# FFN of a two-layer encoder: the gate and the up product of a row block alternate matmul by matmul

## What is computed

```python
def swiglu(h, w_gate, w_up, w_down):
    return (jax.nn.silu(h @ w_gate) * (h @ w_up)) @ w_down

x = x + swiglu(rms_norm(x, f_norm_g[layer]), f_w_gate[layer], f_w_up[layer], f_w_down[layer])
```

## Time and profile before

| | us |
|---|---|
| median of 3 runs | 1744.21 (1743.7 to 1746.51) |
| span of the profiled execution, first to last instruction | 1737.0 |
| difference: around the span | 7.2 |
| PE busy in the span | 1649.4 (95%) |
| DVE, ACT, POOL busy | 776.2 (45%), 622.6 (36%), 228.3 (13%) |
| the twenty looped panels of layer 0, from the trace | 571 to 789 |

### The profile page before, as it was taken

One profiled execution on the slowest core, in us unless ns is written; L12 is line 12 of the kernel. 1 busy time (PEld: TensorE's weight loads), 2 busy tenths in 40 slices (PEclk: granted clock), 3 DMA queues, 4 the chain that ended last, 5 costly groups with the idle time before them and its releaser, 6 DMA issues.

```text
span 1737.0 us, 22605 instructions
## 1 busy us (share of the span) xinstructions
PE 1649.4 (95%) x9358; PEld 1345.0 (77%) x9358; DVE 776.2 (45%) x1011; ACT 622.6 (36%) x1006; POOL 228.3 (13%) x305
## 2 busy tenths in 40 slices
PE   5989989999999999999999997899999999999999
PEld 4778788777768788888888885478776878888887
DVE  4668345453534444442234437835343454444222
ACT  6543333353524322221114335634452432222110
POOL 3853134010000211110000000000000021111000
PEclk9999999999999999999999998999999999999999
DMA  6611012134112333332223221214311233333221
GB/s 208 124 49 50 25 52 75 49 130 137 49 49 73 97 97 97 97 97 97 97 97 98 97 97 37 86 49 145 122 49 49 73 97 97 97 97 97 97 97 73
DMA packets 146801, 151.85 MB, mean 87 GB/s; under 512 B 8864, under 2 KB 109344, under 8 KB 146592
## 3 DMA queue, kind: packets, MB, share of 16 engines
q1 hardware_dynamic: 146720, 150.69, 28.2%
HBM read 147.53 MB, written 3.15 MB: 87 GB/s over the span
## 4 chain that ended last, share of the span: by engine, by line
PE 87%; DVE 7%; ACT 3%; issue 2%; DMA 0%; SPq 0%; POOL 0%; DVEq 0%; ACTq 0%
PE ps L325 24%; PE ps L327 24%; PE ps L326 24%; PE ps L1640 2%; PE ps L1617 1%; PE ps L1996 1%; DVE sb L602 1%; PE ps L956 1%; DVE w_lo_ab L297 1%; DVE sb L2066 1%; ACT w_hi L293 1%; PE ps L1234 1%; PE ps L417 1%; ACT sb L2038 1%; PE ps L1245 1%
## 5 line engine op out<-in xcount | busy, mean ns | idle before, releaser
L325 PE MATMUL ps<-h_hi,w_hi 128*128 128x512 f32 x864 | 337.4, 390 | 4.2 <-DVE w_lo L1810 3.9
L326 PE MATMUL ps<-h_lo,w_hi 128*128 128x512 f32 x864 | 336.2, 389 | 0.0
L297 DVE TENSOR_TENSOR w_lo<-raw,w_hi 128x2048 fp32r<-128x2048 f32 x70 | 160.4, 2292 | 389.8 <-ACT w_hi L293 389.8
L293 ACT ACTIVATE w_hi<-raw 128x2048 fp32r<-128x2048 f32 x84 | 160.7, 1914 | 430.3 <-PE ps L327 429.7
L327 PE MATMUL ps<-h_hi,w_lo 128*128 128x512 f32 x704 | 273.9, 389 | 0.0
L325 PEld LDWEIGHTS ps<-h_hi,w_hi 128*128 128x128 f32 x864 | 162.2, 188 | 38.5 <-issue 5.2
L326 PEld LDWEIGHTS ps<-h_lo,w_hi 128*128 128x128 f32 x864 | 162.2, 188 | 33.3
L1810 DVE TENSOR_TENSOR w_lo<-raw,w_hi 128x2048 fp32r<-128x2048 f32 x44 | 138.1, 3138 | 53.5 <-ACT w_hi L1792 53.5
L327 PEld LDWEIGHTS ps<-h_hi,w_lo 128*128 128x128 f32 x704 | 132.1, 188 | 27.7
L1792 ACT ACTIVATE w_hi<-raw 128x2048 fp32r<-128x2048 f32 x44 | 84.3, 1916 | 160.9 <-PE ps L327 160.9
L325 PE MATMUL ps<-w_hi,a_hi 128*128 128x512 f32 x352 | 137.3, 390 | 1.7 <-DVE up L1808 1.7
(11 more groups left out here) (370 smaller groups left out, 2667.8 us busy)
## 6 DMA issues: line engine op xcount, KB each, us to landing
raw<-in_f_w_gate SPq DMA_DIRECT2D x44, 512.0 KB, 4.0
raw<-in_f_w_up SPq DMA_DIRECT2D x44, 512.0 KB, 5.2
raw<-in_f_w_down SPq DMA_DIRECT2D x44, 512.0 KB, 4.2
raw<-in_xa_w_kv SPq DMA_DIRECT2D x16, 1024.0 KB, 5.0
raw<-in_c_w_qkv SPq DMA_DIRECT2D x12, 1024.0 KB, 5.1
raw<-in_ab_w_in SPq DMA_DIRECT2D x10, 1024.0 KB, 5.8
raw<-in_xa_w_q SPq DMA_DIRECT2D x8, 1024.0 KB, 5.0
raw<-in_xa_w_out SPq DMA_DIRECT2D x8, 1024.0 KB, 5.0
```

The source lines that it names most:

```text
L293: a.activation(w_hi[:, n % 2, :], raw[n % 2], ACT.Copy).then_inc(sem("w_hi"), 1)
L297: v.tensor_tensor(w_lo(n)[:, n % 2, :], raw[n % 2], w_hi[:, n % 2, :].bitcast(F32), ALU.subtract).then_inc(sem("w_lo"), 1)
L325: pe.matmul(out, a[0], b[0], start=start, stop=False)
L326: pe.matmul(out, a[0], b[1], start=False, stop=False)
```

## The change

Inside the loop, the two groups of a panel become one sequence of 24 pairs. For each of the eight blocks of the contraction and each of the three parts, the gate's matmul is followed by the up's, with the same streamed operand, each into its own bank. The number of matmuls, their operands, the banks and the waits at a panel's head stay. The gate's last matmul (which raises `f_mm`) is now the last but one of the panel. The two panels ahead of the loop are as before, and no other engine's code changes.

```diff
+            def both(s):
+
+                for k in range(KT):
+                    for part, (a, b) in enumerate(((0, 0), (0, 1), (1, 0))):
+                        for gu in range(2):
+                            ins = pe.matmul(ps[:, 2 * s + gu, :], weights(s)[a][:, k, gu * P:(gu + 1) * P], hT[b][:, k, :],
+                                            start=k == 0 and part == 0, stop=k == KT - 1 and part == 2)
+                            if k == KT - 1 and part == 2:
+                                done(ins, gu)
+
             with pe.Fori(1, FT // 2) as j:
                 for s in range(2):
                     pe.wait_ge(sem("w_lo"), j * 2 + (nth(n0) + s + 1))
                     pe.wait_ge(sem(f"f{l}_free"), j * 2 + after(f"f{l}_free", s + 1))
-                    for gu in range(2):
-                        done(group(s, gu, range(KT)), gu)
+                    both(s)
```

## The result

The changed kernel takes 1750.39 us (median; 1749.9 to 1752.6) against 1744.21 us: **slower, ratio 1.0037, 95% interval 1.0025 to 1.0050**. That is 6.2 us where 2.2 were forecast, outside the stated range by 0.5 us and beyond the 0.2% that counts as no change. Its profiled execution has a span of 1748.1 us.

What follows compares the result with a forecast made beforehand. The prediction took PE alone to bound the looped panels. Spacing and evacuation at 0 plus loop ends of 1.11 and 1.12 us, added to 1744.21, gave 1746.5 us, counted as the same; range 1743.7 to 1749.9 us.

Steps and rivals of the forecast that it cites:

- Spacing: Looped panels' 1920 matmuls: start-to-start time on PE stays 0.2266 us, 0 us, with 1.6 us either way.
- A: Rival: alternation moves the loop's matmuls closer together, worth 16.5 us, giving 1730.0 us; chance 0.06.
- D: Rival: alternating banks makes the clock swing, one dip per looped panel, 68 us, giving 1814.5 us; chance 0.02.
- Evacuation of each panel: Behind each looped panel: later scaling, silu and weight rounding stay hidden, spare time falls from 5.6 to 4.6 us; 0 us.
- Rival C: In the loop: weights come late if each panel's chain grows by over 4.6 us; 40 us per microsecond beyond; chance 0.03.
- End of the loop: Ahead of each layer's down product: PE also waits for scaling and silu, +1.11 us in layer 0, +1.12 in layer 1.
- the sum: Whole kernel: 1.11 + 1.12 = +2.2 us from the two loop ends, everything else 0.
- rival B: Clock falls behind the longer wait at the loop ends: 1748.2 us with one dip, 1749.9 with two; chance 0.09.
- The later stages: Behind the loop PE runs on unchanged to the last stores, so both shifts stay and nothing is added.
- The base: Starting time: median 1744.21 us, with the profiled span of 1737.0 us taken as 7.2 us under it, untouched.

Runs made afterwards that it cites:

- experiment 2: Changed kernel, but the last looped panel of each layer has the gate's group ahead of the up's again: 1744.7 us, ratio 1.0005.
- experiment 3: Kernel before, but only the last of the loop's 20 panels in each layer alternates gate and up: 1750.94 us, ratio 1.0033.
- experiment 5: Down product's first 12 matmuls, on banks 4 to 7, moved ahead of its wait: kernel before 1742.96 us, ratio 0.9988; changed kernel 1743.31 us, ratio 0.9990.
- experiment 4: Changed kernel, unchanged, timed again beside the kernel before with more executions: 1751.29 us, ratio 1.0034.
- experiment 9: Kernel before with 9, 12, 15, 19 or 20 extra matmuls ahead of layer 0's down product: 1747.05 to 1748.74 us, ratios 1.0008 to 1.0022.

## Why the prediction was wrong, step by step

**Spacing: right.** 0 us forecast; 217.88 against 217.91 us for 960 matmuls. Rivals A and D fall with the same row, D because the clock is 1.00 while the banks alternate at every matmul. The Trainium skill tells of a bf16 kernel in which cycling through banks in each iteration went with small idle times of PE and a swinging clock ("TensorE: Matmul & The Clock Gate", section "A second HAM failure mode: psum-queue depth-cycling"). This loop shows nothing of it: that row has no swing in 960 matmuls.

**Evacuation of each panel: right.** The chain stays hidden. The weights come 4.3 us early instead of 4.6; the 0.3 us are the longer `w_lo`, whose overlap with `a_lo` the forecast did not reckon with. Rival C falls.

**End of the loop: right in size, +1.10 and +1.19 us** for the +1.11 and +1.12 of the sum, and experiments 2, 3 and 5 show that the whole loss hangs on it.

**What failed first is rival B's weight.** The forecast's sum left the clock out and gave a dip behind the longer wait a chance of 0.09; the price of one dip, 1.7 us, was near to the 1.6 measured. In all four profiles of kernels that keep PE idle for 2.03 us at the end of layer 1's loop, the dip is there, 1.6 us each time; where the wait is filled, or 0.84 us long, it is not. My argument against it was one row: no dip behind the 2.5 us ahead of layer 1's loop. That row came from an execution that was 5.8 us shorter than the next profile of the same kernel. The four waits of 2.66 us at L1629 pointed the right way. In the trace of the kernel before, two of them have a dip behind them, the one of the earlier trace rows and the last of these three, and two have none:

```profile
470.00:480.00 10.00, 9.19 (x42) 6.50 (x43) 4.63 (x6) 5.43 (x20) 0.00 (x0) 1.00 0.00 0
1292.00:1302.00 10.00, 8.98 (x41) 6.31 (x42) 4.84 (x6) 5.36 (x19) 0.00 (x0) 1.00 0.00 0
1306.00:1315.00 9.00, 6.79 (x23) 4.26 (x24) 8.03 (x10) 3.56 (x12) 0.00 (x0) 0.81 0.23 75
```

**The later stages, put at nothing, failed as well.** The sum took them over unchanged, since no instruction of theirs is touched. In the profiles of the changed kernel, layer 1's cross-attention takes 1.4 us and the chunk attention 0.5 us longer with the same instructions. Filling the waits does not remove the 1.4, so the idle time at the loops' ends is not its cause. A shift of the stage in either direction goes with it in 12 profiles of 14, but why is not shown.

**The sum, corrected:** 2.3 us of waiting, 1.6 for the dip and 1.9 in later stages make 5.8 in all, against 6.2 us measured first and 5.8 in experiment 4. The first two terms are shown by experiments. The third is seen in the profiles only, and its cause stays open: in experiment 9 a pure delay brought the longer cross-attention in three profiles of five, but no total clearly above the delay.

**The base.** Joining a span of one execution to the median of others made 7.2 us of time around the span; it is 1.8. That did not move the forecast, but it hid the sign that would have warned me: the profiled execution lay at the short end of its kernel's spread.

## What to carry to other kernels

Reordering inside a loop that one engine bounds can be free in the steady state and still cost at the seam, where the next stage waits for what the loop's last pass evacuates: cost the last pass by itself, and give the next stage something to do that does not need it. Here the first 12 matmuls of the down product, on banks the loop does not use, cover the seam and make the order irrelevant (experiment 5). Price a standstill of TensorE of about 2 us at its length plus a possible dip of the clock (1.4 to 1.6 us here), and never argue against a dip from one profiled execution.

## What the runs showed of the hardware

- At a granted clock of 1.00 a 128x512 matmul of this operand type starts 0.227 us after the one before, whether both add into one bank or alternate between two, and whether the stationary or the streamed operand repeats.
- An idle time of 2.03 us between two long stretches of matmuls brought the granted clock down in four of four profiles (layer 1), one of 1.94 us in none of four (layer 0), one of 3.04 us in both layers in the one profile taken. The wait of 2.66 us at L1629 brought it down in two cases of four in the first profile of the kernel before, and the wait of 2.5 us ahead of layer 1's loop in 14 of the 17 profiles. So length alone does not decide. The Trainium skill says in "TensorE: Matmul & The Clock Gate", section "What's actually happening", that the check of TensorE's activity runs free, without starting anew when a kernel starts; the differing outcomes of nearly equal delays in experiment 9 agree with that.
- Twelve executions of one program spread over 1739.7 to 1745.3 us of span, with mean clocks of 0.986 to 0.988; the longest have the lowest clock. With 11 or 12 executions against 21 to 35 of the kernel before, the intervals reach 1.6 to 2.1 us to either side, so a difference of 2 us is only just told from none.
- `w_lo` on DVE takes 3.12 to 3.18 us in the looped panels of the kernel before and 3.25 to 3.42 in those of the changed kernel, each time 2.15 us plus the time for which it overlaps `a_lo` on POOL (0.97 to 1.28 us).
